# A mixture-of-experts block: rows scattered to expert blocks in DRAM ahead of the loop and gathered behind it, instead of gathers and scatters within it

## The reference

```python
logits = xt @ router_w + router_b            # xt: (512, 1024), 32 experts
top_val, top_idx = lax.top_k(logits, 4)      # four experts per token
gates = softmax(top_val)
# the rows of each expert are collected in blocks xb; for each block with expert e:
hcat = xb @ w1[e] + b1[e]                    # w1[e]: (1024, 2048)
h_glu, h_lin = split(hcat); h_glu = minimum(h_glu, 7); h_lin = clip(h_lin, -7, 7)
act = h_glu * sigmoid(1.702 * h_glu) * (h_lin + 1)
y = act @ w2[e] + b2[e]                      # w2[e]: (1024, 1024)
# out[token] = sum over its four experts of gate * y, added to the residual, then a last norm
```

## Time and profile before

| | |
|---|---|
| median of three runs | 1745.91 us |
| the profiled execution, own time | 1745.26 us |
| its span, first to last instruction | 1743.5 us |
| TensorE matmul busy | 1625.8 us, 93% |
| VectorE, ScalarE, GpSimd busy | 580.7, 424.6, 434.4 us |
| read from and written to DRAM | 474.61 MB, 16.86 MB |
| mean granted TensorE clock | 0.962 |

### The profile page before, as it was taken

How to read it: one execution, slowest core, us unless ns; L and a number is a source line. 1 busy time by engine, 2 the same in 40 slices (tenths; PEclk the granted TensorE clock), 3 DMA queues, 4 the chain that set the end, 5 groups by cost and what they waited for, 6 DMA issues and landing times.

```text
span 1743.5 us, 38524 instructions
## 1 busy us (share of the span) xinstructions
PE 1625.8 (93%) x16302; PEld 935.6 (54%) x16302; DVE 580.7 (33%) x1103; ACT 424.6 (24%) x697; POOL 434.4 (25%) x465
## 2 busy tenths in 40 slices
PE   5999998997999849999999999999999999999990
PEld 5999986775779814433433443443443443443340
DVE  3779885213224313112212212211311311221225
ACT  5322122454322322121221221211212212122121
POOL 5344333344243331211211111111121121121122
PEclk8999998999999769999999999999999999999995
DMA  6222322221166338999999999999999999999956
GB/s 175 73 82 89 97 74 66 67 86 49 46 233 233 113 114 352 387 399 403 388 395 400 394 388 400 400 379 402 398 379 401 398 386 400 404 386 398 404 195 245
DMA packets 139580, 482.92 MB, mean 277 GB/s; under 512 B 17141, under 2 KB 66461, under 8 KB 106036
## 3 DMA queue, kind: packets, MB, share of 16 engines
q1 hardware_dynamic: 130404, 464.98, 69.6%
q0 software_dynamic: 8992, 16.85, 2.9%
q10 hardware_dynamic: 144, 0.52, 0.1%
HBM read 474.61 MB, written 16.86 MB: 282 GB/s over the span
## 4 chain that ended last, share of the span: by engine, by line
PE 88%; DVE 4%; issue 2%; DMA 2%; POOL 2%; ACT 1%; SPq 1%; ACTq 0%; POOLq 0%; DVEq 0%
PE banks L1261 38%; PE banks L930 25%; PE banks L1317 19%; PE banks L1305 2%; DVE banks L1412 2%; PE banks L1244 1%; DVE h_res L1648 1%; POOL slot_table L603 1%; PE banks L1281 1%; SPq L370 1%; DMA y_in<-y_rows 0%; DMA small<-in_b_in_dram 0%; ACT h_tok L814 0%; DVE mix_lo L1534 0%; DMA xs<-u_rows,token_now 0%
## 5 line engine op out<-in xcount | busy, mean ns | idle before, releaser
L1261 PE MATMUL banks<-w_ring,xT 128*32 128x512 f32 x6144 | 673.3, 594 | 1.1 <-ACT xT L874 1.1
L1261 PEld LDWEIGHTS banks<-w_ring,xT 128*32 128x32 f32 x6144 | 197.1, 110 | 435.4 <-issue 426.8
L1317 PE MATMUL banks<-w_ring,actT 128*32 128x256 f32 x6144 | 344.8, 380 | 0.0
L1317 PEld LDWEIGHTS banks<-w_ring,actT 128*32 128x32 f32 x6144 | 193.1, 110 | 129.9 <-issue 5.4
L544 POOL TENSOR_TENSOR w_lo<-stage,w_hi 128x2048 fp32r<-128x2048 f32 x40 | 184.3, 4608 | 303.6 <-ACT w_hi L679 303.6
L1618 DVE TENSOR_TENSOR hid<-banks,bias 128x512 f32<-128x512 f32 x96 | 66.4, 692 | 523.8 <-PE banks L1261 523.8
L930 PE MATMUL banks<-u_hi,w_hi 128*128 128x264 f32 (+1 forms) x544 | 184.0, 338 | 11.8 <-ACT gates L768 9.3
L930 PE MATMUL banks<-u_hi,w_lo 128*128 128x264 f32 (+1 forms) x544 | 182.2, 335 | 0.0
L930 PE MATMUL banks<-u_lo,w_hi 128*128 128x264 f32 (+1 forms) x544 | 181.9, 334 | 0.0
L1412 DVE SCALAR_TENSOR_TENSOR banks<-conv_in,taps,banks 128x512 f32<-128x512 f32 x224 | 150.9, 748 | 0.0
L1641 DVE TENSOR_TENSOR y_out<-banks,bias 128x256 f32<-128x256 f32 x96 | 40.8, 425 | 296.4 <-PE banks L1317 296.4
(11 more groups left out here) (242 smaller groups left out, 1639.6 us busy)
## 6 DMA issues: line engine op xcount, KB each, us to landing
w_ring<-in_expert_w_dram SPq DMA_DIRECT2D x384, 1024.0 KB, 10.5
stage<-in_w_in_dram SPq DMA_DIRECT2D x20, 1024.0 KB, 5.3
stage<-in_w_in_dram SPq DMA_DIRECT2D x16, 512.0 KB, 5.3
y_in<-y_rows SPq DMA_DIRECT2D x3, 2048.0 KB, 13.0
stage<-in_conv_pw_w_dram SPq DMA_DIRECT2D x4, 1024.0 KB, 5.1
stage<-in_mlstm_out_w_dram SPq DMA_DIRECT2D x4, 1024.0 KB, 5.2
stage<-in_w_out_dram SPq DMA_DIRECT2D x4, 1024.0 KB, 5.3
x_sb<-in_x_dram SPq DMA_DIRECT2D x4, 512.0 KB, 7.0
```

The costliest lines, as they stand in the source:

```text
L1261: last = nc.tensor.matmul(banks[32 * g:32 * (g + 1), t].rearrange("p (h n) -> p h n", h=2), xT[:, k, 32 * t:32 * (t + 1)], w1_ring[k][:, : ...
L1317: last = nc.tensor.matmul(banks[32 * g:32 * (g + 1), 3 + t, 0:GRP], actT[:, k, 32 * t:32 * (t + 1)], w2_ring[k // 2][:, k % 2, GRP * g:GRP ...
```

## The change

Rows move through DRAM in the order of the slots. Ahead of the loop GpSimd scatters the rows of `u2` themselves, 16 indirect transfers of 128 rows of 4 KB, to `x_slots` (block, slot, row); the blocks were filled with zeros by ScalarE's queue during the first projections. Within the loop the rows of a block are loaded by SP and the results stored by ScalarE's queue with plain transfers of all 96 slots, in a layout in which partition 32g + s holds columns 256g to 256g + 255 of slot s. VectorE's transpose of 32 x 32 blocks turns them into stationary operands (`turn_rows`, and one transpose for each part of the activated rows), which takes the place of TensorE's transposes and ScalarE's copies. A piece b of w1 must then hold the rows 256g + 32b + j on partition 32g + j, and the hidden units are taken by the products in a strided order so that the second product's operand comes out right. Behind the loop GpSimd gathers the results with 16 indirect transfers. `u2` has four buffers, the stores of `u2` and the table are gone, and the norm's gain vector `gf_bc` has a place of its own and is loaded directly behind the router's weights.

```diff
+        x_slot = nc.dram_tensor("x_slots", [(PASSES * NE + 1) * SLOTS, D], F32).ap()
+        y_slot = nc.dram_tensor("y_slots", [NE * SLOTS, D], F32).ap()
+        def slot_rows(rows, n, t):
+            return rows.rearrange("(m s) (g c) -> m g s c", s=32, g=CG)[bass.ds(n * TG + t, 1)].rearrange("o g s c -> (o g) s c")
...
@@ SP
                 if c < W1C:
-                    src = expert_w1[0, bass.ds(e, 1), P * c:P * (c + 1), :].rearrange("e p (g n) -> p (e g) n", g=2)
-                    sp.dma_start(w1_ring[c], src).then_inc(ring_in[c], 16)
+                    src = expert_w1[0, bass.ds(e, 1)].rearrange("e (g b j) n -> b (e g) j n", g=CG, j=32)[c]
+                    sp.dma_start(w1_ring[c].rearrange("p h n -> p (h n)"), src).then_inc(ring_in[c], 16)
...
+            def load_rows(n):
+                for t in range(TG):
+                    sp.dma_start(xs[:, GRP * t:GRP * (t + 1)], slot_rows(x_slot, n, t)).then_inc(xs_in, 16)
+            sp.wait_ge(rows_sent, 16 * TT * TOPK)
+            load_rows(0)
+            sp.wait_ge(xT_made, 1)
+            load_rows(1)
             def load_block(n, e):
                 for c in range(RING):
+                    if c == W1C:
+                        sp.wait_ge(xT_made, n + 1)
+                        load_rows(n + 1)
...
@@ GpSimd, ahead of and behind the loop
-                pool.indirect_dma_start(out=table, out_offset=bass.IndirectOffsetOnAxis(ap=dest[:, m:m + 1], axis=0),
-                                        in_=code[:, m:m + 1], in_offset=None).then_inc(table_written, 16)
+                pool.indirect_dma_start(out=x_slot, out_offset=bass.IndirectOffsetOnAxis(ap=dest[:, m:m + 1], axis=0),
+                                        in_=u2[:, m // TOPK], in_offset=None).then_inc(rows_sent, 16)
...
+                pool.wait_ge(y_stored, (q + 1) * (16 * TG * NE) + 1)
+                carry_wait()
+                for m in range(TT * TOPK):
+                    pool.indirect_dma_start(out=y_in[:, m // TOPK, m % TOPK], out_offset=None, in_=y_slot,
+                                            in_offset=bass.IndirectOffsetOnAxis(ap=y_row[:, m:m + 1], axis=0),
+                                            bounds_check=last_row, oob_is_err=False).then_inc(y_loaded[m], 16)
...
@@ ScalarE
+                act.dma_start(first_slots[:, EMPTIED * ct:EMPTIED * (ct + 1)],
+                              empty_row.unsqueeze(1).to_broadcast([P, EMPTIED, GRP])).then_inc(slots_emptied, 16)
...
+                    for t in range(TG):
+                        act.wait_ge(y_made, n * TG + (t + 2))
+                        act.dma_start(slot_rows(y_slot, e, t), y_out[:, t]).then_inc(y_stored, 16)
...
@@ TensorE
-                            last = nc.tensor.matmul(banks[32 * g:32 * (g + 1), t].rearrange("p (h n) -> p h n", h=2),
-                                                    xT[:, k, 32 * t:32 * (t + 1)], w1_ring[k][:, :, GRP * g:GRP * (g + 1)],
+                            units = w1_ring[k].rearrange("p h (b g j) -> p g (h b) j", g=CG, j=32)[:, g]
+                            last = nc.tensor.matmul(banks[32 * g:32 * (g + 1), t].rearrange("p (c j) -> p c j", j=32),
+                                                    xT[:, t, k], units, start=k == 0, stop=k == KT - 1, tile_position=(0, 32 * g))
...
-                    transposes(0)
-                    transposes(1)
-                    x_transposes(n + 1)
-                    second(0)
-                    transposes(2)
-                    second(1)
-                    second(2)
+                    for t in range(TG):
+                        second(t)
...
@@ VectorE
+            def turn_rows(n):
+                dve.wait_ge(xs_in, (n + 1) * (16 * TG))
+                nc.vector.transpose(xT.rearrange("p t k s -> p (t k s)"), xs).then_inc(xT_made, 1)
...
-                        nc.vector.tensor_tensor(act_v[:, t], lin, sig[:, t], ALU.mult).then_inc(act_made, 1)
+                        own(nc.vector.tensor_tensor(act_v[:, t], lin, sig[:, t], ALU.mult))
+                        nc.vector.transpose(actT[:, t].rearrange("p k s -> p (k s)"), act_v[:, t]).then_inc(actT_made, 1)
```

More of the change, by code:

```diff
@@ L79 @@
 PARTS = 3
-NONE = 1 << 14
 RING = 12
@@ L198, in under_ring @@
             return at(name, shape, dt, off)
-        w_router = under_ring("w_router", [P, KT, NE])
-        logits = under_ring("logits", [P, TT, NE])
+        gf_bc = under_ring("gf_bc", [P, D])
+        w_router, _ = take("w_router", [P, KT, NE])
+        logits, _ = take("logits", [P, TT, NE])
+        empty_row, _ = take("empty_row", [P, GRP])
+        assert top[0] <= limit, (top[0], limit)
         rb_bc = under_ring("rb_bc", [P, NE])
@@ L1205, in row_transposes @@
                         col = P * (4 * f + k)
-                        last = nc.tensor.transpose(banks[:, 4 * (1 - i % 2) + f, P * k:P * (k + 1)], u2[:, i % 2, col:col + P], ident)
+                        last = nc.tensor.transpose(banks[:, 4 * (1 - i % 2) + f, P * k:P * (k + 1)], u2[:, i, col:col + P], ident)
                     last.then_inc(u2_mm, 1)
@@ L1238, in _ @@
             places(TT)
-            def x_transposes(n):
-                pe.wait_ge(xs_in, (n + 1) * 16)
-                for k in range(KT):
-                    last = nc.tensor.transpose(banks[:, k // 4, SLOTS * (k % 4):SLOTS * (k % 4 + 1)], xs[:, P * k:P * (k + 1)],
-                                               ident[0:SLOTS, 0:SLOTS])
-                last.then_inc(xs_used, 1)
-            pe.wait_ge(wo_out, 2 * TT)
-            x_transposes(0)
+            pe.wait_ge(mask_made, TT)
             pe.wait_ge(bias_split, PARTS + 3)
@@ L1296, in _ @@
                         last.then_inc(hid_mm, 1)
-                    def transposes(t):
-                        pe.wait_ge(act_made, n * TG + (t + 1))
-                        if t >= 2:
-                            pe.wait_ge(actT_made, n * TG + (t - 1))
-                        for h in range(2):
-                            last = nc.tensor.transpose(banks[:, 6 + t % 2, P * h:P * (h + 1)], act_v[:, t, P * h:P * (h + 1)], ident)
-                        last.then_inc(act_mm, 1)
                     def second(t):
-                        pe.wait_ge(bias_made, n * 3 + 3)
+                        if t == 0:
+                            pe.wait_ge(y_made, n * TG + 1)
                         pe.wait_ge(actT_made, n * TG + (t + 1))
@@ L1569, in find_slots @@
                 chain(nc.vector.tensor_reduce(place[:, i], picked[:, i], axis=AX.X, op=ALU.add))
-                nc.vector.scalar_tensor_tensor(out=dest[:, TOPK * i:TOPK * (i + 1)], in0=place[:, i], scalar=float(NE), in1=expert_f[:, i],
+                chain(nc.vector.tensor_tensor(late[:, i], steps96.unsqueeze(1).to_broadcast([P, TOPK, PASSES - 1]),
+                                              place[:, i].unsqueeze(2).to_broadcast([P, TOPK, PASSES - 1]), ALU.is_le))
+                chain(nc.vector.tensor_reduce(in_pass[:, i], late[:, i], axis=AX.X, op=ALU.add))
+                chain(nc.vector.scalar_tensor_tensor(out=place[:, i], in0=in_pass[:, i], scalar=-float(SLOTS), in1=place[:, i],
+                                                     op0=ALU.mult, op1=ALU.add))
+                chain(nc.vector.scalar_tensor_tensor(out=local[:, i], in0=expert_f[:, i], scalar=float(SLOTS), in1=place[:, i],
+                                                     op0=ALU.mult, op1=ALU.add))
+                nc.vector.scalar_tensor_tensor(out=dest[:, TOPK * i:TOPK * (i + 1)], in0=in_pass[:, i], scalar=float(NE * SLOTS), in1=local[:, i],
                                                op0=ALU.mult, op1=ALU.add).then_inc(dest_made, 1)
```

237 lines of the change are left out of this document (88 added, 149 removed).

## The result

The changed kernel takes 3831.66 us, median of four runs (3828.43 to 3853.47); the kernel before took 1745.47 on the same chip. The ratio is 2.1978, interval 2.1936 to 2.202. The profiled execution took 3828.43 us, its span is 3826.7 us. The forecast was 3813 us. A kernel's executions can fall into a faster and a slower group, and the ratios in this text, each with a 95% interval, compare the faster groups alone, so they are not exactly quotients of the medians.

What follows compares the result with a forecast made beforehand. TensorE bounds the loop before, transfers close behind; after the change, four DMA engines carrying w1 do. Loop +2052, ahead +16, behind -1 sum to +2067 on 1745.9: 3813 us, range 3470 to 4200.

Steps and rivals of the forecast that it cites:

- the first step: Loads of w1: a transfer is divided along its outermost count, so 4 gives four of 16 DMA engines.
- The rate of one engine: DMA transfers: one engine moves 26.0 GB/s for 8 KB rows, 25.2 for 4 KB, 22.2 for 1 KB.
- the upper bound of 4160 us: Loop: alternating with y rows slows weights to 19.0 GB/s per engine, 11 us more per block, +340.
- The block: One expert-loop block on the four engines carrying w1: 99.9 us, against 33.2 before.
- The split of the remainder: Block time beside w1's 80.7 us: w2 10.4 us on all 16 engines, x 4.4 and y 4.4 on four.
- my lower bound: Loop: x and y rows cost the four engines nothing, 91.1 us per block, -273; with no delay ahead about 3510.
- Ahead of the loop: Before the expert loop: routing starts some 24 us late, 8 us saved, sum +16 us.
- the queue: Before the loop: slow w1 pieces delay the projection's weights and gain vector, so routing starts some 24 us late.
- Behind the loop: After the loop: 16 gathers replace five loads, final scaling follows all sums; -1 us, between -6 and +8.
- Case 2: Loads of w1: all 16 engines carry them after all, faster, 1698 us; chance 0.11.
- Case 3: Loop: 16 engines, but y stores slow the weights as the scatters do, 1786 us; chance 0.03.
- Case 4: Loads of w1: one engine carries them, 323 us per block, about 11700 us; chance 0.02.

Runs made afterwards that it cites:

- E1: Kernel before, only w1's source taken in 4 groups of 32 far-apart rows: 3829.36 us.
- E3: Kernel before, only w1's source taken in 8 groups of 16 rows: 2890.04 us.
- E2: Kernel before, only w1's source taken in 16 groups of 8 rows: 2426.55 us.
- E10: Changed kernel with x loads and y stores each issued as four transfers, w1 left as it is: 3868.84 us.
- E11: Changed kernel with w1 read in neighbouring rows, the scattered rows' columns permuted instead, x and y still counting 4: 1930.03 us.
- E12: Changed kernel with w1 in neighbouring rows, scattered rows' columns permuted, and x loads and y stores each issued as four transfers: 1754.66 us, ratio 1.0002.
- E7: Kernel before, each w1 piece as four transfers of 32 neighbouring rows into 32 neighbouring partitions: 2488.14 us.
- E4: Changed kernel with every w1 and x load and y store issued as four transfers, each counting 32: 2256.48 us, ratio 1.2877.
- E9: Kernel before, each w1 piece as four transfers of 32 rows, each taking every fourth row and writing every fourth partition: 1745.68 us.
- E8: Kernel before with act transposed by VectorE and TensorE reading w1's columns in matching order, all transfers unchanged: 1715.19 us, ratio 0.983.

## Why the prediction was right, and where its steps were off

**The mechanism, and the first step.** "It is divided along its outermost count", with 4 giving four engines: shown by E1 (the line alone, 3829) and by the share of 0.25 with 106 GB/s. E1, E3 and E2 fall in order with 4, 8 and 16 groups, but E3 and E2 stay far above what the count alone gives.

**The rate of one engine.** I had 26.0 GB/s for rows of 8 KB; the w1 stretch has 106 / 4 = 26.5, and the rows of y among the pieces do not lower it, so the 19.0 GB/s from which the upper bound of 4160 us was worked out did not come about. w1's share of the block is 8.389 MB / 106 GB/s = 79.1 us, I had 80.7.

**The block.** 99.9 us predicted, 98.98 measured in the steady stretch. The loop from its first product to the end of its last took 3095 us, I had 3116.

**The split of the remainder holds in the changed kernel, but not the conclusion from it.** The four engines' part of a block lasts 86 us: w1, x and y are 9.18 MB, which at 106 GB/s are 86.6 us, so x and y take 7.4 us there, and I had 8.8. The rest, 98.98 - 86.6 = 12.4 us, is w2, and I had 10.4. The two misses nearly cancel. But E1 has no plain x and y rows on the four engines, and its period is 97.15, that of the changed kernel 97.0; my terms give 91.1, and with my wider bounds for E1 93 to 97. And E10, which takes these rows off the four engines, has (3738.8 - 693.7) / 31 = 98.2. So my lower bound, "if the x and y rows cost those engines nothing", could not be reached by freeing the four engines of them. Cut into stretches of 1 us between 1300 and 1700, a share of at most 0.32 (four engines at work) stands in 73% of E1's time and 75% of E10's, against 87% in the changed kernel (1274 to 1670): the part of the four engines does get shorter, and the other part gets longer, from about 13 us a block to about 25. With x and y on four engines and all 16 carrying w1, E11 was worked out as 39.4 us and has 38.9 over all, and spreading x and y (E12) takes 5.4 off. What fills the gap in E1 and E10 shows in one stretch of each, in which TensorE waits and SP issues w2:

```profile
2042.00:2063.00 21.00, 0.00 (x0) 0.00 (x0) 0.00 (x0) 0.00 (x0) 0.00 (x0) 0.57 0.74 187
```
```profile
1370.00:1386.00 16.00, 0.00 (x0) 0.00 (x0) 0.00 (x0) 0.00 (x0) 0.00 (x0) 0.50 0.67 181
```

There a busy engine moves 187 / 0.74 / 16 = 15.8 and 181 / 0.67 / 16 = 16.9 GB/s, where I took 25.2 for w2's rows: at such a rate 0.262 MB would need 15.5 to 16.6 us, not 10.4. That w2 starts while the four engines still have w1 before them, and that the engines then get in each other's way where they write, would fit E7, but it is only argued; the cause stays open.

**Ahead of the loop: the term that was mis-sized.** I had +16, it is +47: the first product starts at 684.9, not 637.7. The first pair of the projection was late as said, and by 12 us more (its weights land at 558, I had 546). What I missed is how long SP itself stands in these issues. SP's issues by time:

```profile
498.66 17.94 SPq L414 DMA_DIRECT2D w_ring<-in_expert_w_dram  x4
516.65 17.69 SPq L369 DMA_DIRECT2D stage<-in_w_out_dram  x2
534.38 22.73 SPq L414 DMA_DIRECT2D w_ring<-in_expert_w_dram  x2
...
585.62 21.91 SPq L418 DMA_DIRECT2D w_ring<-in_expert_w_dram  x4
607.58 6.62 SPq L437 DMA_DIRECT2D w_router<-in_router_w_dram  x1
614.24 9.66 SPq L438 DMA_DIRECT2D rb_bc<-in_router_b_dram  x1
623.94 0.46 SPq L439 DMA_DIRECT2D gf_bc<-in_norm_ffn_g_dram  x1
```

Before, SP's first four pieces took 2.12 us to issue; now 17.94. The gain vector, which I put near 608, is issued at 623.94 and lands at 633.4, and the chain of waits goes through it:

```profile
623.94 9.50 DMA gf_bc<-in_norm_ffn_g_dram
633.47 1.30 DVE u L1477
...
683.82 0.99 DVE xT L1537
684.94 7.81 PE banks L1206 x48
```

All of this comes from w1's pattern: in E11 the first product starts at 636.4, 1.3 us earlier than in the kernel before. So what the rest of the change saves there is 1.3 us, not my 8, and the queue costs 48, not 24.

**Behind the loop.** I had -1; from the end of the last product to the end of the span it is 3826.7 - 3779.5 = 47.2 us against 41.3, +6, inside my -6 to +8. The row loads of 8.49 us have given way to 16 gathers of 990 to 2035 ns, one after the other, and the last lands 6.12 us after its issue. The sum of the three terms is +2030 + 47 + 6 = +2083, and 1743.5 + 2083 is the span. I had +2052 + 16 - 1 = +2067. So the loop came out 22 us shorter and the other two terms 38 us longer than forecast: the mechanism is right, but that the total is off by only 0.5% is partly luck.

**The rivals.** Case 2 was rightly unlikely, but its price was wrong twice over. It says that with 8 engines a block would take 55 us; E3 with eight groups has 68.2. And 16 engines alone do not bring 1698 us: E2 and E4, which have them, take 2427 and 2256. E12, which has the engines and the spread for w1, takes 1755. Case 3, the y stores in the way, has nothing to show for it in the changed kernel, where w1 runs at 106 GB/s with y's rows and without them. Case 4 is excluded by the share; its 11700 us don't follow from what it states: 31 x (323 - 33.2) + 1746 is 10730, and with w2, x and y on the same engine about 12150.

## What to carry to other kernels

Before a load's pattern is rearranged so that a later step becomes simpler, read off its outermost count on both sides and which partitions are written together: here one line of `rearrange` turned 1745 us into 3829. A permutation is cheaper where little data passes (the scattered rows, in four VectorE operations) than in the 8 MB that are streamed for each expert. And take a change apart before judging it: one of its parts alone was worth 1.7%.

## What the runs showed of the chip that I had not expected

- All 16 engines busy is not full rate. At shares of 0.93 the loop ran at 221 to 229 GB/s when a transfer was dealt in 16 groups of eight neighbouring partitions, or filled only 32 neighbouring ones; 394 when the 32 were every fourth. Four engines with 32 neighbouring partitions each lose nothing: 26.5 GB/s for each.
- A shortage on four engines travels: while they lag, SP stands up to 20 us in a single issue, also in that of small loads that come behind, such as the router's bias (9.66 us).
- SP can issue four times as many w1 transfers (1024 in place of 256) at no cost that can be seen: E9 takes 1745.68 us in its one run.
- The transfers did not hold a faster TensorE back at the 394 GB/s they had before: E8 ran them at 405.
